# Moving the tie-breaking of one prompt tile from ahead of the attention loop into its first groups

## What is computed

```python
score = where(causal, einsum(iw, relu(einsum(iq, ik))), -inf)
_, idx = lax.top_k(score, topk)          # topk = 256
logits = q . k[idx] * HEAD_DIM ** -0.5   # 8 heads, 2 key/value heads
p = softmax(logits); o = p . v[idx]
```

## Time and profile before

| | us |
|---|---|
| median of 3 runs | 1305.14 (1304.88 to 1307.22) |
| the profiled execution | 1305.35 |
| its span, first to last instruction | 1303.6 |
| PE busy | 1263.4 (97%) |
| DVE busy | 857.0 (66%) |
| POOL busy | 733.3 (56%) |
| ACT busy | 670.5 (51%) |

### The profile page before, as it was taken

One profiled execution on the slowest core, in us unless ns is written; L12 is line 12 of the kernel. 1 busy time (PEld: TensorE's weight loads), 2 busy tenths in 40 slices (PEclk: granted clock), 3 DMA queues, 4 the chain that ended last, 5 costly groups with the idle time before them and its releaser, 6 DMA issues.

```text
span 1303.6 us, 25268 instructions
## 1 busy us (share of the span) xinstructions
PE 1263.4 (97%) x9537; PEld 1159.3 (89%) x9537; DVE 857.0 (66%) x1586; ACT 670.5 (51%) x1151; POOL 733.3 (56%) x473
## 2 busy tenths in 40 slices
PE   6899999999899999999999999999999999999998
PEld 4677999877766766999999999999999999999998
DVE  5777889889678848677973454555545553644595
ACT  5557988967777776455342343433334336211115
POOL 0242457990152103456587787887878857765620
PEclk8899999999899999999999999999999999999999
DMA  9722106542101127655322243523534268999633
GB/s 347 281 70 74 50 6 213 173 143 82 46 21 30 46 74 228 191 158 146 106 98 66 99 167 133 186 101 130 185 134 170 78 248 311 328 334 347 242 129 131
DMA packets 127274, 198.86 MB, mean 153 GB/s; under 512 B 16839, under 2 KB 100111, under 8 KB 116656
## 3 DMA queue, kind: packets, MB, share of 16 engines
q1 hardware_dynamic: 127008, 193.01, 43.0%
q10 hardware_dynamic: 144, 4.23, 0.8%
HBM read 144.07 MB, written 53.18 MB: 151 GB/s over the span
## 4 chain that ended last, share of the span: by engine, by line
PE 70%; DVE 8%; ACT 5%; POOLq 5%; POOL 3%; DVEq 2%; issue 2%; SPq 2%; ACTq 1%; DMA 1%
PE ps L3508 30%; PE ps L3528 15%; PE ps L3192 2%; PE ps L3206 2%; PE ps L3372 2%; ACT junk L1354 2%; PE ps L3374 2%; PE ps L3373 2%; PE ps L3181 1%; POOLq L1076 1%; DMA ada_shift<-in_ada_w 1%; DVE junk L2073 1%; PE ps L3182 1%; DVEq L2623 1%; PE ps L3325 1%
## 5 line engine op out<-in xcount | busy, mean ns | idle before, releaser
L3528 PE MATMUL ps<-input,down_H 128*128 128x258 f32 x1120 | 180.7, 283 | 1.5 <-DVE acc L2771 1.5
L3528 PEld LDWEIGHTS ps<-input,down_H 128*128 128x128 f32 x1120 | 154.5, 190 | 2.1 <-issue 1.1
L3508 PE MATMUL ps<-comb,opH 128*128 128x258 f32 x960 | 154.4, 283 | 0.0
L1170 POOL TENSOR_TENSOR opL<-wsum,opH 128x512 fp32r<-128x512 f32 x80 | 123.7, 1556 | 36.1 <-ACT opH L1690 32.7
L1690 ACT CAST opH<-wsum 128x512 fp32r<-128x512 f32 x80 | 49.6, 621 | 168.0 <-PE ps L3508 109.6
L3508 PEld LDWEIGHTS ps<-comb,opH 128*128 128x128 f32 x960 | 132.7, 190 | 0.0
L3508 PE MATMUL ps<-h2H,opH 128*128 128x258 f32 x640 | 129.0, 283 | 0.3 <-DVE h2L L2628 0.3
L3508 PE MATMUL ps<-h2H,opL 128*128 128x258 f32 x640 | 129.0, 283 | 0.0
L3508 PE MATMUL ps<-h2L,opH 128*128 128x258 f32 x640 | 128.6, 282 | 0.0
L1013 POOL TENSOR_TENSOR wL<-wraw,wH 128x1024 fp32r<-128x1024 f32 x28 | 70.1, 2504 | 86.9 <-ACT wH L1347 86.7
L2771 DVE TENSOR_TENSOR acc<-ps,acc 128x516 f32<-128x516 f32 x112 | 76.6, 694 | 61.7 <-PE ps L3528 61.2
(11 more groups left out here) (528 smaller groups left out, 3532.1 us busy)
## 6 DMA issues: line engine op xcount, KB each, us to landing
down_inputs<-staged SPq DMA_DIRECT2D x35, 1032.0 KB, 4.9
input<-down_inputs SPq DMA_DIRECT2D x35, 1032.0 KB, 7.1
adb<-in_ada_w SPq DMA_DIRECT2D x8, 2048.0 KB, 8.5
wraw<-in_w_out SPq DMA_DIRECT2D x24, 512.0 KB, 4.5
raw<-in_w_gate SPq DMA_DIRECT2D x10, 1024.0 KB, 6.5
raw<-in_w_up SPq DMA_DIRECT2D x10, 1024.0 KB, 5.2
down_block<-in_w_down SPq DMA_DIRECT2D x5, 2048.0 KB, 11.0
x_feature_major<-x0T ACTq DMA_DIRECT2D x1, 4128.0 KB, 15.2
```

The costliest lines, as they stand in the source:

```text
L1170: pool.tensor_tensor(opL[g % OPS][:], operand(v, p), opH[g % OPS][:].bitcast(F32), ALU.subtract).then_inc(s_wL, 1)
L3508: ins = mm(ps[:, sum_bank(v, p) + h, 0:HC], weight[s][:, k, :], token[:, k, h * HC:(h + 1) * HC], start=begins, stop=ends, skip_group_chec ...
L3528: ins = mm(ps[:, 2 * m + h, 0:HC], weight[:, f, cc], tok[:, f, part, h * HC:(h + 1) * HC], start=(f == 0 and weight is hi and part == 0), ...
```

## The change

`EARLY_TIES` goes from 4 to 3, so entry 3 (768 keys) is no longer among the early ones, and its four steps ahead of the loop are taken out. `TIE_AT` gets a row for it in front: steps in groups 1, 2, 3 and 3. The row of entry 4 (896 keys) changes from (2, 4, 5, 6) to (4, 4, 5, 6): its step 0 moves from group 2 to group 4, in front of its step 1. The rows of entries 5 and 6 stay. Entry 3 now uses `late_eq` and `late_pre`.

```diff
-EARLY_TIES = 4
+EARLY_TIES = 3
 EARLY_W = P * (FIRST_SEL + EARLY_TIES)
-TIE_AT = ((2, 4, 5, 6), (6, 7, 10, 10), (12, 12, 13, 13))
+TIE_AT = ((1, 2, 3, 3), (4, 4, 5, 6), (6, 7, 10, 10), (12, 12, 13, 13))
...
             gated(2)
             gated(3)
-            ties(3)
             root_input(2)
             root_input(3)
             ada_row_late(ADA_1 + 7)
```

## The result

The changed kernel takes 1309.02 us (median of 18 runs, 1307.04 to 1310.98) where the kernel before takes 1306.01 us (18 runs, 1304.33 to 1309.23). The ratio is 1.0019 with a 95% interval of 1.0012 to 1.0027: 2.5 us more, 1.6 to 3.5 (the two medians themselves lie 3.0 apart). So it is slower by a little: the interval leaves out "no change", but 0.2% is about the least that can be told here. The forecast was +1.8 us. Of all executions told of here, one of the last kernel took 1748.44 us at a granted clock of 0.653 and is left out.

What follows compares the result with a forecast made beforehand. PE was taken as the bound, waiting in groups 2 and 4 on the chain from DVE's place over POOL. Terms 0 + 0 + 1.1 + 0.4 + 0.3 gave +1.8 us, a median of 1306.9 us, range 1304.2 to 1309.2.

Steps and rivals of the forecast that it cites:

- Part 1: Ahead of the loop: taking out entry 3's steps is worth 0 us, between 0 and -1.2, as root_input(2) then waits for ACT.
- I am wrong if the first logits move: Loop start: PE's first logits were to stay at 338.9; if they moved, the prediction was wrong.
- Group 1: Entry 3's step 0 (0.61 us) fits DVE's idling, or waits for POOL's inverse_diagonal and later idling absorbs it: 0 us.
- Group 2: Entry 3's step 1, a scan, holds POOL's converted(1), delaying q_stacked and PE: +1.1 us, bounds 0 and +1.3.
- a sum higher by 0.2: Group 2: by the skill's page the scan would wait out POOL's inverse_diagonal, making the sum 0.2 us higher.
- Group 3: Entry 3's steps 2 and 3 (2.24 us) make DVE's place(3) late beyond PE's shift: +0.4 us, bounds 0 and +1.2.
- Group 4: Entry 4's step 0 (0.77 us) runs ahead of its step 1; the scan still keeps POOL from q_stacked: +0.3 us.
- The sum: Whole kernel: 0 + 0 + 1.1 + 0.4 + 0.3 = +1.8 us, a median of 1306.9 us, chance 62%.
- PE full: Groups 5 and 6 onward: old order, only shifted; PE, busy throughout 385 to 390, gives none of the shift back.
- at the end too: Sign: the shift is 1.8 us at 390 and still 1.8 us at the kernel's end.
- the forecast's own case: The parts' bounds together give 1305.2 to 1308.4 us around the forecast of 1306.9, chance 62%.
- The clock rival: Longer PE idling at 362.31 and 374.56 drops the clock to 0.50 between 362 and 385: +2.5 us, 1309.4, chance 13%.

Runs made afterwards that it cites:

- the last kernel: Kernel before with PSUM zero as group 4 scan's second input, q_stacked ahead of converted on POOL, scan(1) ahead of last_keys_low: 1304.69 us, ratio 0.9981.
- the second profiles: Changed kernel and kernel before, both run again without an edit: 1308.63 us against 1307.35, ratio 1.0011.
- the PSUM zero: Early tie scans read a PSUM zero as second input: on the changed kernel (groups 2, 4) ratio 0.9998 to before, on the kernel before (group 4) 1.0004.
- the two kernels without group 8's wait: Kernel before and changed kernel, each with scan(1) ahead of last_keys_low on DVE in group 8: 1305.00 and 1306.63 us, ratios to before 0.9977 and 0.9996.
- before, PSUM zero, q_stacked first: Kernel before with a PSUM zero as group 4 scan's second input and q_stacked ahead of converted on POOL: ratio to before 0.9997.

## Why the prediction was right, and where it was not

**Part 1, 0 us: right.** root_input(2) now waits for ACT, 4.00 us where some 3.5 were said: in this profile ACT's square is 1.71 us later, DVE's list ahead of the wait only 1.16. From the end of that wait's cause to the first logits nothing moved: ACT's square to the first logits is 338.89 - 325.61 = 13.28 us before; after, with

```profile
327.32 1.06 ACT L1403 ACTIVATE spare<-decay 128x1032 f32<-128x1032 f32 x1
```

it is 340.61 - 327.32 = 13.29. The stated sign "I am wrong if the first logits move" was badly chosen, since they move by up to 4.5 us from profile to profile with the start of the kernel. The distance was the thing to name.

**Group 1, 0 us: nearly.** The step waited for POOL and took 1.35 us, near the upper bound. The idling hid most of it, but place(1) came 0.15 us later (359.48 against 357.61, less 1.72), and 0.07 in the second profiles; POOL passed it on to PE.

**Group 2, +1.1 us: right, mechanism and size.** converted(1) takes 1.94 us against the 0.87 of the earlier trace rows, as forecast ("about 1.9"), 1.07 us more. With place(1)'s 0.15 it is the shift of 1.23 that PE shows, and with 0.07 the 1.13 of the second profiles. That the scan does it, and by its second input from SBUF, is shown by the PSUM zero: the same scan beside the same instruction, 0.62 us.

The Trainium skill ("SBUF — State Buffer", section "Who interferes with whom") says that a VectorE instruction with at most one SBUF input, in no two-port mode, leaves GpSimd alone, and that one with two excludes GpSimd's reads. The runs agree, with the numbers above. Its other rule, that whoever issues first keeps the port, gave a sum higher by 0.2. In group 2 the scan is 0.17 us longer (1.93 against 1.76 of the earlier trace rows) with inverse_diagonal's last 0.3 us beside it, and in group 4 it is 0.36 longer (2.38 against 2.02 of the earlier trace rows) with a conversion that began first. So POOL does hold a scan that comes later, as the Trainium skill says, though for less than the whole overlap (0.32 and 0.51 us). The sum did not need it.

**Group 3, +0.4 us.** place(3) came at 371.39, 30.78 us behind the first logits; in the kernel before it was 29.28 behind:

```profile
368.17 0.42 DVE L2303 TENSOR_TENSOR attT<-ps,inverse_diagonal 128x256 f32<-128x256 f32 x1
```

That is +1.50, or 0.27 beyond PE's shift of 1.23. The term was right in kind and a little too large.

**Group 4, +0.3 us.** The order was the one forecast: tensor_scalar, conversion, scan, and the scan keeps POOL from q_stacked. PE's wait is 1.49 us; the forecast said about 1.7. The moved step 0 by itself did nothing to PE's wait (0.99 against 1.03). Groups 3 and 4 together were forecast at +0.7 and came to 1.68 - 1.23 = +0.45. Without steps 2 and 3 these 0.5 us are gone, so the rest of 0.18 in group 4 comes from the late place(3) too: the tensor_scalar then goes ahead of converted(2) and makes it longer. The 0.3 was on the wrong account, and somewhat too much.

**The sum, +1.8 us: right.** It is 1.68 and 1.57 in the two profiles at the second q_transposed, and 1.63 in time and 1.5 in the trace between the two kernels without group 8's wait. "From there on with PE full nothing gives it back" holds up to group 8, where the shift is still 1.69. The sign "at the end too" did not hold: there it is 3.28.

**The range: in part luck.** The median of 1309.02 lies 2.1 us above the forecast of 1306.9 and 0.2 under the upper end of 1309.2. Of the 2.1, 0.9 is the kernel before, whose 18 runs have a median of 1306.01 where the 3 runs at hand had 1305.14. The range reaches so far up only because it leaves room for a fall of the clock, and the fall that came was not the one it had in mind. The lower bound of the forecast's own case, 1305.2, is not the sum of the parts' bounds either: group 2 stands in it with 1.1, although its lower bound is 0. Nothing hung on that here.

**What the prediction did not see** is group 8. The clock rival was in the list, and its mechanism was right: PE idles, the granted clock falls to 0.50, some us are lost. Its place and condition were wrong. It was to be decided "between 362 and 385", where the change lengthens PE's idling; there the clock stayed at 1.00 behind waits of 1.41 and 1.49 us. It fell behind a wait of 2.09 us that the change does not lengthen, and cost 1.6, not 2.5 us: 3.4 us at 0.50 cost about half of their length here, while the 2.5 was close to the whole of the 3 us that it assumed. The view was at hand: a wait of 2.09 us, twice the one ahead of the loop's half clock, stood in the trace before, and the sentence "PE full" rested on 385 to 390 alone. A shift does not only pass through later waits, it also moves them.

**What stays open.** Why that wait drops the clock in some kernels and not in others. It has the same length in all of these, 2.09 or 2.10 us; its place behind the first logits differs:

| kernel | the wait ends, us behind the first logits | granted clock behind it |
|---|---|---|
| before, PSUM zero, q_stacked first | 67.91 | 1.00 |
| changed, PSUM zero | 68.82 | 0.50 |
| before, PSUM zero | 68.93 | 0.50 |
| before, entry 4's step 0 in group 4 | 69.13 | 1.00 |
| before, both profiles | 70.03 | 1.00 |
| changed, converted(1) in group 3 | 71.02 | 1.00 |
| changed, without steps 2 and 3 | 71.05 | 1.00 |
| changed, both profiles | 71.60, 71.72 | 0.50 |

So it is neither later nor earlier that decides: kernels without a fall stand on both sides of the two at 68.8 to 68.9, and 0.2 us lie between a fall and none (68.93 and 69.13). That the place decides at all is not shown; the kernels differ in their edits as well. The two whose loop began with a half clock of 6.8 us do without the fall, but so do three kernels with 10.2. No row ties the fall to the steps that are moved, other than by their shift. How many of the timed runs have the fall is not seen: the profiles of the two kernels differ by 3.2 to 3.3 us behind the first logits, the timed runs by 2.5 and 1.4.

## What to carry to other kernels

Before work is put into idle gaps of one engine, look at what the neighbour that shares a port runs at that time: it is not the 1.76 us of the scan on DVE that cost, since DVE had room, but the 1.07 us by which it held POOL, on which PE already waited. An operand that need not come from SBUF (a constant column in PSUM) takes such a hold away without moving anything. And a shift should be followed to the end of the loop: list every long wait of PE behind it, for the clock may fall behind one that the shift has only moved, and the wait can perhaps be taken away, as here by one pair of steps in the other order.

## What the runs showed of the hardware

- A scan whose second input is one PSUM column read again for each element runs as fast as with SBUF (1.75 and 2.02 us for 768 and 896 columns) and leaves POOL free: 0.62 and 0.61 us beside it instead of 1.94 and 2.21.
- A tensor_scalar on DVE and a POOL instruction also hold each other up: 1.35 instead of 0.61 us in group 1 behind inverse_diagonal, and POOL's conversion 1.13 instead of 0.72 in group 4 beside it.
- The same 2.09 us of idling on PE halved the clock for some 3.4 us, at a price of 1.5 to 1.6 us, or did not, and did so alike in two profiles of the same kernel.
- The time up to the loop varies by 4.5 us between profiles of nearly the same program, so a difference of 1 or 2 us is read from distances inside the trace, not from its span.
